# Two loads cut into six-row transfers, and the last two pairs of experts loaded in single 2 MB chunks

## The reference

```python
def expert_block(args):                       # for every expert e and its rows xb
    xb, e = args
    gu = xb @ w_gate_up[e] + b_gate_up[e]     # w_gate_up[e]: 1024 x 2048 float32, 8 MB
    gate, up = gu[..., :D_FF_EXPERT], gu[..., D_FF_EXPERT:]
    gate = jnp.minimum(gate, SWIGLU_LIMIT)
    up = jnp.clip(up, -SWIGLU_LIMIT, SWIGLU_LIMIT)
    act = (up + 1.0) * gate * jax.nn.sigmoid(SWIGLU_ALPHA * gate)
    return act @ w_down[e] + b_down[e]        # w_down[e]: 1024 x 1024 float32, 4 MB
```

## Time and profile before

| | us |
|---|---|
| median of three executions | 1192.5 |
| the profiled execution | 1192.38 |
| its span in the trace | 1190.7 |
| TensorE matmuls busy | 1105.9 (93% of the span) |
| VectorE busy | 350.4 (29%) |
| ScalarE busy | 167.0 (14%) |
| loads on SyncE's queue, share of 16 DMA engines over the span | 86.7% |

### The profile page before, as it was taken

How to read it: one execution, slowest core, us unless ns; L and a number is a source line. 1 busy time by engine, 2 the same in 40 slices (tenths; PEclk the granted TensorE clock), 3 DMA queues, 4 the chain that set the end, 5 groups by cost and what they waited for, 6 DMA issues and landing times.

```text
span 1190.7 us, 15332 instructions
## 1 busy us (share of the span) xinstructions
PE 1105.9 (93%) x6539; PEld 539.3 (45%) x6539; DVE 350.4 (29%) x740; ACT 167.0 (14%) x272; POOL 4.0 (0%) x23
## 2 busy tenths in 40 slices
PE   7999999999999999999898799998799898989897
PEld 5889886763434343433332334333334333333332
DVE  4685234463312212212222122212112212121313
ACT  3431234441100000010101000101010101010002
POOL 1000000000000000000000000000000000000000
PEclk9999999999999999999998899999899999999999
DMA  9832414677999999999999999999999999999994
GB/s 336 302 142 72 141 71 116 279 280 302 429 426 429 427 427 431 432 430 428 429 430 429 427 428 431 428 433 425 428 429 432 428 432 427 434 424 435 423 427 170
DMA packets 39053, 436.04 MB, mean 366 GB/s; under 512 B 5813, under 2 KB 5898, under 8 KB 20330
## 3 DMA queue, kind: packets, MB, share of 16 engines
q1 hardware_dynamic: 37066, 433.67, 86.7%
q10 hardware_dynamic: 1920, 1.34, 0.6%
HBM read 433.95 MB, written 1.05 MB: 365 GB/s over the span
## 4 chain that ended last, share of the span: by engine, by line
PE 65%; DMA 31%; issue 2%; DVE 1%; ACT 1%; SPq 0%; DVEq 0%; PEldq 0%
DMA ring<-in_w_down 27%; PE ps L1970 19%; PE ps L2010 16%; PE ps L1548 4%; PE ps L1659 4%; PE ps L2025 3%; PE ps L1605 3%; DMA ring<-in_w_gate_up 3%; PE ps L1940 3%; PE ps L1528 3%; PE ps L1655 2%; PE ps L1716 2%; PE ps L1792 1%; PE ps L1836 1%; DMA ring<-in_w_in 1%
## 5 line engine op out<-in xcount | busy, mean ns | idle before, releaser
L2010 PE MATMUL ps<-ring,work 128*64 128x512 f32 x1024 | 238.2, 613 | 32.0 <-DMA ring<-in_w_down 27.8
L1970 PE MATMUL ps<-work 128*64 128x512 f32 x1024 | 234.4, 600 | 0.2 <-DVE work L1394 0.2
L1970 PE MATMUL ps<-ring,work 128*64 128x512 f32 x1024 | 225.5, 593 | 8.2 <-DMA ring<-in_w_gate_up 8.2
L2010 PEld LDWEIGHTS ps<-ring,work 128*64 128x64 f32 x1024 | 78.5, 140 | 166.6 <-issue 155.0
L1970 PEld LDWEIGHTS ps<-ring,work 128*64 128x64 f32 x1024 | 72.5, 137 | 156.4 <-issue 141.9
L1970 PEld LDWEIGHTS ps<-work 128*64 128x64 f32 x1024 | 73.9, 139 | 138.7 <-issue 132.1
L1427 DVE COPY work<-ps 128x512 f32<-128x512 f32 x16 | 11.1, 691 | 241.6 <-PE ps L1528 241.6
L1404 DVE TENSOR_SCALAR work<-ps 128x512 f32<-128x512 f32 x32 | 22.0, 686 | 196.3 <-PE ps L1528 196.3
L1439 DVE COPY work<-ps 128x512 f32<-128x512 f32 (+1 forms) x16 | 11.1, 691 | 206.4 <-PE ps L2010 206.4
L787 ACT ACTIVATE ps<-work 128x512 f32<-128x512 f32 x32 | 19.3, 602 | 365.1 <-DVE work L1404 365.1
L2025 PE MATMUL ps<-work 128*128 128x512 f32 (+1 forms) x132 | 59.7, 608 | 10.4 <-ACT work L794 10.2
(11 more groups left out here) (237 smaller groups left out, 722.4 us busy)
## 6 DMA issues: line engine op xcount, KB each, us to landing
work<-in_w_gate_up SPq DMA_DIRECT2D x64, 2048.0 KB, 34.6
ring<-in_w_gate_up SPq DMA_DIRECT2D x24, 4096.0 KB, 31.8
ring<-in_w_down SPq DMA_DIRECT2D x22, 4096.0 KB, 35.7
ring<-in_w_down SPq DMA_DIRECT2D x19, 2048.0 KB, 21.7
ring<-in_w_gate_up SPq DMA_DIRECT2D x16, 2048.0 KB, 20.0
ring<-in_w_in SPq DMA_DIRECT2D x7, 2048.0 KB, 15.5
ring<-in_xattn_w_kv SPq DMA_DIRECT2D x2, 2048.0 KB, 13.8
ring<-in_w_out SPq DMA_DIRECT2D x2, 2048.0 KB, 8.2
```

Of the source, the lines that this page charges most:

```text
L1970: last = nc.tensor.matmul(bank(b)[p], xg_T[k][:, kb, :], quad_columns(w[:, kk, D_MODEL * (q // 2):D_MODEL * (q // 2 + 1)], q % 2), start=F ...
L2010: last = nc.tensor.matmul(bank(Y_BANK + y)[p], act_T[k][:, b, HALF * c:HALF * c + HALF], w[:, b, 512 * q:512 * q + 512], start=False, stop ...
```

## The change

Two things change, both in what SyncE issues for the last three pairs.

First, chunk 0 of pair 13 and chunk 0 of pair 14 are each loaded by nine transfers instead of one: eight of six rows (rows 0 to 5, 6 to 11, ... 42 to 47) and one of the remaining 80 rows. All nine raise the same semaphore, and `loads_by_sixes` adds eight to the count that TensorE waits for.

Second, `by_halves` becomes true for all chunks of pairs 14 and 15. Their twins are no longer loaded as 4 MB but chunk by chunk, each with its own slot wait and its own semaphore. The order of the chunks stays 0 to 11, and the last chunk keeps its four pieces.

```diff
+ENDING = 2
+BY_SIXES = [(13, 0), (14, 0)]
+SIXES, SIX_ROWS = 8, 48
...
         def by_halves(i, c):
-            return i < BY_HALVES or (i == PAIRS - 1 and c >= 8)
+            return i < BY_HALVES or i >= PAIRS - ENDING
...
+        def loads_by_sixes(i, s):
+
+            return SIXES * len([1 for j, c in BY_SIXES if j <= i and chunk_place(j, c)[0] == s])
...
-            return uses_before_experts(s) + use
+            return uses_before_experts(s) + use + loads_by_sixes(i, s)
...
-                sp.dma_start(place(s), src).then_inc(S(f"slot_loaded{s}"), 16)
+                if isinstance(i, int) and (i, c) in BY_SIXES:
+                    for r in range(0, SIX_ROWS, 6):
+                        sp.dma_start(place(s)[r:r + 6], src[r:r + 6]).then_inc(S(f"slot_loaded{s}"), 16)
+                    sp.dma_start(place(s)[SIX_ROWS:], src[SIX_ROWS:]).then_inc(S(f"slot_loaded{s}"), 16)
+                else:
+                    sp.dma_start(place(s), src).then_inc(S(f"slot_loaded{s}"), 16)
...
-            for i in range(PAIRS - TURN_PAIRS, last):
+            for i in range(PAIRS - TURN_PAIRS, PAIRS - ENDING):
                 load_pair(i, i, lambda use: use, lambda use: use)
-            load_pair(last, last, lambda use: use, lambda use: use, range(8))
-            for c in (8, 9, 10):
-                load_half(last, c)
+            for i in range(PAIRS - ENDING, PAIRS):
+                for c in range(PAIR_CHUNKS):
+                    if (i, c) != (last, 11):
+                        load_half(i, c)
```

More of the change, by code:

```diff
@@ L383, in loads_in_first_pass @@
         def loads_in_first_pass(s):
-            return uses_before_experts(s) + len([1 for i in range(PAIRS) for c in range(PAIR_CHUNKS)
-                                                 if chunk_place(i, c)[0] == s and first_pass_chunk(i, c)[1] is not None])
+            return uses_before_experts(s) + loads_by_sixes(PAIRS, s) + len(
+                [1 for i in range(PAIRS) for c in range(PAIR_CHUNKS)
+                 if chunk_place(i, c)[0] == s and first_pass_chunk(i, c)[1] is not None])
         def later_pass_place(c):
```

## The result

The changed kernel takes 1229.1 us (median of four executions, 1224.0 to 1231.9) against 1192.5 us before: a ratio of 1.030 (95% interval 1.0265 to 1.0334), 36.6 us more. Slower was forecast, but by 9 us, and the time lies outside the range.

A forecast was written before the change was run, and what follows sets the result against it. DMA engines were taken as the bound from about 283 us until the weights end. 1192.4 - 0.3 (single chunks) + 9.4 (six-row loads) = 1201.5 us, range 1188.2 to 1213.

The forecast's parts named there:

- the single chunks: Pairs 14 and 15: 2 MB transfers cost 0.4 us, earlier landings win at most 0.7; 0.3 us gained.
- The issuing step: SyncE issues nine transfers instead of one, 3.4 us more per load, hidden by queued work; cost 0.
- the last link: End of the stream: after chunk 10 lands, 7.1 us for last two chunks, combination and norm, as before.
- 3.1: Six-row loads: us the six engines need beyond 11.5 per load, with five of the 80 rows each at full rate.
- the 10 us of lead: Six-row loads: the six engines lead by 10 us, subtracted from their 19.4 us, leaving 9.4.
- rival D: Six-row loads: no narrow-write loss, but the six include lagging engines; +6.1 us, 1198.2 us; without lead 1211.5; chance 0.08.
- A: Six-row loads: rows share ways in, a third of the rate; 1207.8, in series 1218.9; 0.17 with rival D's second form.
- B: Six-row loads: no narrow-write loss, six leading engines, lag levelled; last landings 3.7 us earlier, 1188.4 us; chance 0.29.
- C: Six-row loads: some loss, just paid by the lead; nothing moves by more than 2.4 us, 1192; chance 0.13.
- some 10 us: Sign around 1000 and 1055: GB/s clearly below 430 for this long, DMA share staying 1.0.
- 5 us and more: Sign: TensorE waits this long for chunk 0 of pairs 13 and 14.
- The half-empty stretch at the end: Sign at the stream's end: the time with about half the engines done, up to 10 us before, gets shorter.

The follow-up runs named there:

- e5: Changed kernel, but of chunk 0 of pairs 13 and 14 only rows 48 to 127 are loaded; 1207.4 us, +15.4 against the kernel before.
- e7: Changed kernel, but chunk 0 of pairs 13 and 14 comes as two transfers of 64 neighbouring rows; 1222.3 us, +30.2 against the kernel before.
- e13: Changed kernel, but two transfers of 64 neighbouring rows for chunk 0 of pairs 1 and 2, no six-row loads; 1205.7 us, +12.6 against the kernel before.
- e12: Changed kernel, but only chunk 0 of pair 13 is loaded by six-row transfers; 1211.4 us, +19.2 against the kernel before.
- e4: Changed kernel, but the first 48 rows come as one transfer over all 16 engines, then the 80; 1218.2 us, +25.8 against the kernel before.
- e3: Changed kernel, but each six-row transfer takes every fourth row, same 48 rows; 1227.2 us, +34.9 against the kernel before.

## Why the prediction was wrong

The sign was right: six-row transfers into few partitions lose bandwidth, and the single chunks give nothing (-0.3 forecast, -0.7 measured, zero within its interval). The issuing step was right (2.7 us for eight, hidden), and so was the last link (7.1 us behind the last landing). The size failed, 36.6 instead of 9.1 us, in this sum: "The six engines then need 11.5 + 3.1 = 14.6 us instead of 4.9 per load, 9.7 more, 19.4 for both. If they lead by 10 us, 9.4 us are left over".

- The step that failed first is the "3.1", the 80 rows at full rate. The earlier trace rows had shown half the rate for 32 partitions, and I applied it to the 48 rows alone, as if 80 neighbouring rows were a full transfer. Alone they cost 19 us for the two loads (e5), where the sum had nothing.
- The second is that the loss was put on six engines only. The rows of ordinary transfers were slow as well (2.4 us instead of 1.2 for 32 KB in e5). My reading is that two engines which write through one way in are both slow, whatever transfer each is in. So all 16 lose, from the 4 MB in front of the load to those behind it: the stream as a whole is 24 us late (1166 to 1190), and by e7 against e13 a late load of 64 + 64 rows costs up to three times its own half rate.
- The third is the 10 us of lead that were subtracted. That is right only if all of the six lead, and if they alone are slow. The spread in the changed kernel (three engines in front, twelve between, one far behind) fits five of the six among the eight leaders and one among the laggards: this one went from 8.6 to 13.6 us behind the first at the first load, 5.0 us for its 8 extra rows. The two loads cost 19.2 and 17.4 us (e12), not 9.7 and 9.7 less 10.
- The six engines' own part is 10.8 us (e4 against the changed kernel). It falls on one engine that ends far behind the rest. That is rival D's mechanism, a lagging engine among the six, priced there at 6.1 us without other losses. Against the other ten engines the eight extra rows per load are 9.8 us for both. At the second load the last engine fell back by more than its rows explain (from 15.1 to 23.8 us); why stays open. The engine's number isn't in the rows.

Of the rivals A was the nearest (1207.8, strictly in series 1218.9), for its cause too: shared ways in. But it too put the loss on the six engines alone and subtracted the lead, and by it e3 should have helped, which it didn't. B and C fall.

Of the signs: GB/s dropped at both loads at a share of 0.99 and 1.00 (single stretches of 5 us show 0.94 beside 1.07), but for over 25 us each and not for "some 10 us". The waits of "5 us and more" came (8.76, 5.67 and 8.66 us), but for the chunks in front of the load rather than for chunk 0. The half-empty stretch at the end became longer, 24 us instead of 10, and not shorter.

How the 36.6 us come about by the rows: 13.1 + 14.5 = 27.6 us of transfer time in the two dips, of which 5 each are the load's own half rate (as in e13) and the rest, by subtraction, its encounter with the neighbouring transfers; the remaining 9 are what the slowest engine lost beyond the average. Counted from the first engine instead of the average, the same 37 us are 24 and 13.

Open: which engine gets which row of a partial transfer. That 64 neighbouring rows run at half rate on all 16 engines (210 GB/s at a share of 0.97), while even rows run at the full rate, would follow if the engine is chosen by a row's place in the transfer and not by its partition; no view shows the engine. Open too is why e3 is no cheaper than the six neighbouring rows. Its 48 rows still lie in the same twelve groups of four as before; that this is the reason is not shown.

No variant beats the kernel before; the single chunks alone are level with it.

## What to carry to other kernels

In a stream that keeps the DMA engines full, a load could be cut by columns at no cost (+0.2 us), and by rows only so that each part meets all groups of four partitions evenly (every second or fourth row, +0.5 and +0.6 us). A cut into neighbouring rows is to be priced as half rate for all engines and for the transfers before and behind it, not for its own bytes alone. And a DMA share of 1.0 says nothing of the rate: GB/s has to be read beside it.

## What the hardware showed unexpectedly

- 2 MB in two transfers of 64 neighbouring rows: 10 us at 210 GB/s on engines with no backlog, half the full rate; late in the stream 20 us at 223 GB/s and 15 more at 344 (e13, e7).
- A transfer slows the one queued in front of it: chunks issued before the six-row loads came 8.9 us later than before, and rows of 32 KB took 2.4 instead of 1.2 us beside the 80 rows of e5. The engines don't reach a transfer at the same time.
- The 16 engines drift apart in a long stream of equal shares: 2.2 us between first and last at 300 us, 10.8 at the end. In the changed kernel what the loads added stayed: 23.8 us behind the second one, 23.6 at the end.
